# Moving the weight block sums of two seven-product feed-forwards from VectorE to GpSimd

## The reference, cut to what matters

```python
h = rmsnorm(x, norm_ffn[layer])
x = x + (jax.nn.silu(h @ w_gate[layer]) * (h @ w_up[layer])) @ w_down[layer]
```

## Time and profile before

| what | value |
|---|---|
| median of 3 runs | 2076.34 us (2073.32 to 2083.42) |
| the profiled execution: own time | 2077.95 us |
| its span | 2076.2 us |
| mean granted TensorE clock | 0.896 |
| PE busy | 1702.6 us (82%) |
| DVE busy | 706.7 us (34%) |
| ACT busy | 359.4 us (17%) |
| POOL busy | 79.9 us (4%), all before 580 us |
| DMA | 381.57 MB, mean 184 GB/s |

### The profile page before, as it was taken

One profiled execution on the slowest core, in us unless ns is written; L12 is line 12 of the kernel. 1 busy time (PEld: TensorE's weight loads), 2 busy tenths in 40 slices (PEclk: granted clock), 3 DMA queues, 4 the chain that ended last, 5 costly groups with the idle time before them and its releaser, 6 DMA issues.

```text
span 2076.2 us, 31931 instructions
## 1 busy us (share of the span) xinstructions
PE 1702.6 (82%) x14144; PEld 1154.0 (56%) x14144; DVE 706.7 (34%) x1255; ACT 359.4 (17%) x832; POOL 79.9 (4%) x85
## 2 busy tenths in 40 slices
PE   6999889969978585556555688989999889899997
PEld 3665458848962251122111256657994466659963
DVE  2005473362340410000000024464664243546663
ACT  2010213232321220000000022421010124310000
POOL 0000004203300000000000000000000000000000
PEclk7999999978998797788778898989999989899999
DMA  9431120000004959999999961213545522134450
GB/s 375 180 122 41 65 82 3 3 1 3 4 3 182 397 245 427 428 427 428 428 428 428 427 230 47 102 56 116 209 169 197 194 101 82 41 122 168 175 196 21
DMA packets 35164, 381.57 MB, mean 184 GB/s; under 512 B 6674, under 2 KB 10130, under 8 KB 12242
## 3 DMA queue, kind: packets, MB, share of 16 engines
q1 hardware_dynamic: 35028, 379.53, 45.7%
HBM read 378.46 MB, written 1.05 MB: 183 GB/s over the span
## 4 chain that ended last, share of the span: by engine, by line
PE 48%; DMA 11%; DVE 4%; ACT 2%; issue 1%; SPq 0%; DVEq 0%; ACTq 0%
PE psum L2619 14%; PE psum L1764 7%; PE psum L2690 7%; DMA arena<-in_w_moe 6%; PE psum L2055 5%; DMA weight_ring<-in_w_moe 5%; PE psum L2058 3%; PE psum L2210 3%; PE psum L1726 3%; PE psum L2186 1%; PE psum L2165 1%; PE psum L1706 1%; PE psum L2074 0%; ACT arena L2262 0%; PE psum L2151 0%
## 5 line engine op out<-in xcount | busy, mean ns | idle before, releaser
L1764 PE MATMUL psum<-weight_ring,arena 128*32 128x512 f32 x640 | 142.6, 716 | 126.5 <-DMA arena<-in_w_moe 92.2
L1188 PE MATMUL psum<-arena 64*64 64x64 f32 x4608 | 151.4, 223 | 20.3 <-PEq L945 8.2
L2619 PE MATMUL psum<-arena 128*128 128x128 f32 x1408 | 165.2, 275 | 1.7 <-DVE arena L2822 1.7
L2619 PEld LDWEIGHTS psum<-arena 128*128 128x128 f32 x1408 | 161.1, 192 | 2.0 <-issue 2.0
L1188 PEld LDWEIGHTS psum<-arena 64*64 64x64 f32 x4608 | 143.7, 138 | 28.2 <-issue 24.2
L1764 PEld LDWEIGHTS psum<-weight_ring,arena 128*32 128x32 f32 x640 | 35.9, 129 | 204.9 <-issue 204.9
L1899 DVE COPY arena<-psum 128x512 f32<-128x512 f32 x16 | 11.1, 692 | 370.3 <-PE psum L1764 370.3
L2619 PE MATMUL psum<-arena,weight_ring 128*128 128x128 f32 x1056 | 131.9, 283 | 4.7 <-ACT arena L2736 2.6
L1764 PE MATMUL psum<-arena 128*32 128x512 f32 x384 | 107.4, 726 | 34.3 <-DMA weight_ring<-in_w_moe 33.9
L2619 PEld LDWEIGHTS psum<-arena,weight_ring 128*128 128x128 f32 x1056 | 127.3, 199 | 5.9 <-DVE arena L2867 3.1
L2055 PE MATMUL psum<-arena,weight_ring 128*128 128x256 f32 x512 | 123.8, 401 | 0.0
(11 more groups left out here) (491 smaller groups left out, 2250.1 us busy)
## 6 DMA issues: line engine op xcount, KB each, us to landing
weight_ring<-in_w_moe SPq DMA_DIRECT2D x60, 2048.0 KB, 20.2
arena<-in_w_moe SPq DMA_DIRECT2D x36, 2048.0 KB, 20.2
weight_ring<-in_w_in SPq DMA_DIRECT2D x23, 2048.0 KB, 8.4
weight_ring<-in_w_mod SPq DMA_DIRECT2D x12, 2048.0 KB, 8.7
weight_ring<-in_w_gate SPq DMA_DIRECT2D x12, 2048.0 KB, 8.0
weight_ring<-in_w_up SPq DMA_DIRECT2D x12, 2048.0 KB, 7.6
weight_ring<-in_w_down SPq DMA_DIRECT2D x12, 2048.0 KB, 7.6
weight_ring<-in_w_out SPq DMA_DIRECT2D x6, 2048.0 KB, 8.0
```

The lines of the kernel that those rows point to most:

```text
L1188: last = nc.tensor.matmul(K.ps[half[d], bank, column + HD * n:column + HD * n + HD], lhs(d, h), rhs(d, h), start=True, stop=True, skip_gro ...
L1764: last = nc.tensor.matmul(K.ps[strip(j), 4, :], xsT[:, k, CAP * e:CAP * e + CAP], ws[j][:, k, :], start=(k == 0), stop=(k == KT - 1), skip ...
L2619: last = nc.tensor.matmul(K.ps[:, bank, P * n:P * n + P], lhs, rhs, start=(n == 0 and k == 0 and name in ("m1", "m5", "m6")), stop=(k == 3 ...
```

## The change

The sums are issued by GpSimd from a program of its own in this block, slot after slot, all 18 of a layer, from the point at which the mixer's output is ready. DVE's queue loses them: the two early slots at the end of the mixer, the four between the evictions of a unit, and the rest behind the last unit. The formulas and the widths are the same. The wait on the buffer is now on product m3 of slot v - 2; the wait on the landed weights moves with the sums.

```diff
-    def block_sum(dve, v, n):
-        if v >= UNITS + FCH:
-            return
+    def block_sum(pool, v, n):
         slot = START + v
         to = block_sums[:, v % 2]
         if n == 0:
-            W.await_landed(dve, slot)
+            W.await_landed(pool, slot)
             if v >= 2:
-                dve.wait_ge(made, 7 * (v - 1) if v <= UNITS + 1 else 7 * UNITS + v - UNITS - 1)
+                pool.wait_ge(made, step["m3", v - 2] if v <= UNITS + 1 else 7 * UNITS + v - UNITS - 1)
...
         if n in (1, 3):
-            dve.wait_ge(sums_ready, 4 * v + (1 if n == 1 else 2))
+            pool.wait_ge(sums_ready, 4 * v + (1 if n == 1 else 2))
         out, x, y, op = ops[n]
-        nc.vector.tensor_tensor(out, x, y, op).then_inc(sums_ready, 1)
-
-    def early_sums(dve):
-        for v in range(2):
+        nc.gpsimd.tensor_tensor(out, x, y, op).then_inc(sums_ready, 1)
+
+    def gpsimd(pool):
+        pool.wait_ge(K.shared("o_ready"), layer + 1)
+        for v in range(UNITS + FCH):
             for n in range(4):
-                block_sum(dve, v, n)
+                block_sum(pool, v, n)
...
-            if u:
-                block_sum(dve, u + 1, 0)
...
-        for v in range(UNITS + 1, UNITS + FCH):
-            for n in range(4):
-                block_sum(dve, v, n)
-
...
             @block.gpsimd
             def _(pool):
-                pass
+                feed_0[4](pool)
+                feed_1[4](pool)
```

More of the change, by code:

```diff
@@ L2325, in scalar, with vector @@
             item(name)
-    def vector(dve, meanwhile):
+    def vector(dve):
         link = chain(dve, dve_step)
@@ L2543, in vector @@
         ins.then_inc(o_ready, 1)
-        meanwhile(dve)
         for t in range(TT):
@@ L2828, in unit @@
             nc.vector.tensor_tensor(to[2], bank(2), u3[:, par, 0:n], ALU.add).then_inc(took, 1)
-            if u:
-                block_sum(dve, u + 1, 1)
             if par:
@@ L2835, in unit @@
                 nc.vector.tensor_tensor(opened, bank(0), gate[:, c % 2, 0, 0:n], ALU.mult).then_inc(hid_opened, 1)
-            if u:
-                block_sum(dve, u + 1, 2)
             dve.wait_ge(made, step["m4", u])
             nc.vector.tensor_tensor(to[1], bank(1), first[:, par, 0:n], ALU.add).then_inc(took, 1)
-            if u:
-                block_sum(dve, u + 1, 3)
             dve.wait_ge(made, step["m3", u])
@@ L2921, in feed_forward @@
     A.high = top
-    return sync, tensor, scalar, vector, early_sums
+    return sync, tensor, scalar, vector, gpsimd
 def experts_and_layers(nc, K):
@@ L2954, in _ @@
             def _(dve):
[L2955 to L2959, removed]
+                for part in parts:
+                    part[3](dve)
 def first_and_second_block(nc, dram, out):
```

## The result

The changed kernel takes 2164.55 us in the median of 4 runs (2161.51 to 2173.31), the kernel before 2079.88 (2073.32 to 2089.35, 4 runs): a ratio of 1.041, 95% interval 1.0357 to 1.0464. It is slower, at 2165 where 2169 was forecast. The profiled execution took 2164.4 us with a span of 2162.6, which is 86.4 us more than before. The two feed-forwards account for more than that.

The account below looks back on a forecast made before the run. TensorE runs nearly without a break; 5.7 us per layer could be blamed on DVE. Meeting 30.2, clock 13 and pace 3.3 make 46.5 us per layer, 93 for both: 2171 profiled, 2169 us median, range 2082 to 2190.

Parts of the forecast that it names:

- The meeting of the two engines: At odd units' ends GpSimd's sums start while DVE closes the chunk, delaying TensorE's eviction: 30.2 us per layer.
- the upper bound: Each of DVE's five chunk-closing instructions waits for the sum in progress: TensorE loses 6.6 us, 3.8 at unit 10.
- one path for both operands of GpSimd: GpSimd's 2.13 ns per element against DVE's 1.2, read as fetching two operands one after the other.
- The clock: TensorE's granted clock falls behind each of five gaps per layer: 2.6 us per gap, 13 us per layer.
- the tail: Last two down slots: 0.5 us more clock loss per layer behind a longer gap.
- GpSimd's pace: Slower sums delay the first down slot by 0.7 to 1 us and the last two by 1.8.
- What was free was free: Early slots' sums finish before TensorE wants them; four sums, 8.7 us, fit a 12.5 us unit: no cost.
- No contention: Rival: at chunk ends the engines do not delay each other; 3.3 us per layer, 2083 us, chance 0.18.
- blocked once: Rival: at chunk ends DVE waits for the first sum, then runs its five through; 2085 us, chance 0.10.
- half blocked: Rival: at chunk ends DVE gets its turn after two sums, not four; 2118 us, chance 0.13.
- The other side: Rival: GpSimd's 1024-wide sum takes 1.22 us and nothing contends; first down-slot gap goes; 2072.6 us, chance 0.04.

Follow-up runs that it names:

- e5: Changed kernel with one operand of each of VectorE's five chunk-closing instructions taken from an idle PSUM bank: 2087.95 us, ratio 1.0041 to the kernel before.
- e1: Changed kernel with GpSimd waiting before the sums of an odd slot until VectorE has closed the chunk before it: 2093.52 us, ratio 1.0082 to the kernel before.

## Why the prediction was right

**The meeting of the two engines.** The step that I chose without a row for it, the upper bound, was the right one: all four sums run ahead of L2820. The reason that I took from the rows, that 2.13 ns per element point to one path for both operands of GpSimd, is still only a reading: the experiments show which accesses meet, not how GpSimd fetches them. Its size: 4 x 6.2 us and 3.6 more at unit 10 (4.45 against 0.83), 28.5 us per layer for the 30.2 forecast. Two errors went against each other. A 1024-wide sum takes 2.35 us, not 2.18. But a short VectorE instruction between two sums adds less than its own length: with one between them the sums start 2.49 us apart (1451.77 to 1454.26) against 2.31 without (e5: 1446.94 to 1449.26), so 0.18 us for one of 0.42.

**The clock.** Forecast 13.0 us per layer behind the five gaps and 0.5 more in the tail; the lengths leave 12.3 and 1.3. One full gap seen by itself cost 2.5 us, for the 2.6 I took.

**GpSimd's pace.** Forecast 0.7 to 1 us at the first down slot and 1.8 at the last two; measured 1.8 and 2.4. The mis-sized term is the sum's length: 2.35 us wide and 1.26 narrow, where I doubled the 1.09 of the scan. At the first place L2838 and L2843 of unit 11 took turns with the last sums as well.

**What was free was free.** The early slots' sums started at 1388.2 us, and TensorE waited for none of them; throughput holds at 9.4 us of sums for a 12.5 us unit, as e1 shows.

**The rivals.** No contention would have meant about e5's 2088 us for the changed kernel, and not the 2083 of the prediction, which had GpSimd's pace too short and no clock behind it; blocked once and half blocked have fallen by the four stretched instructions. The other side, a wide sum of 1.22 us, fell with 2.35.

The steps add up to 28.5 + 13.6 + 1.8 + 2.4 = 46.3 us per layer, the mean of the two layers, for 46.5 forecast. So near a hit is partly luck: the meeting was 1.7 us too dear, the two places of the pace 1.4 us too cheap (4.2 us where 2.8 were forecast at most). That the time came out 4 us under the forecast is no term of the sum. The two profiled executions differ outside the feed-forwards as well, most of all at the start of the mixer, where TensorE stood nearly idle for 4.5 us in both (0.7 us of matmuls). Windows behind that pause, before and after (columns as in the earlier trace rows):

```profile
1638.40:1646.00 7.60, 7.59 (x17) 3.70 (x18) 1.49 (x4) 1.14 (x3) 0.00 (x0) 0.60 0.97 411
```

```profile
1683.80:1691.00 7.20, 7.16 (x23) 3.79 (x24) 1.77 (x4) 2.32 (x7) 0.00 (x0) 1.00 0.99 422
```

Why the granted clock fell in one and not in the other stays open.

## What to carry to other kernels

Before work goes to GpSimd, list what VectorE runs at that moment by its operands: an instruction with two SBUF inputs, or a fast one with one, takes turns with each GpSimd instruction that reads SBUF. Here that cost up to 6.2 us of gap a chunk, and the 81 us a layer taken off VectorE gave nothing back, since they lay beside the matmuls. If the work must go there, start it at an event at which VectorE only evicts from PSUM, or put it in shorter pieces. And ask first whether the waits blamed on the busy engine can be met by awaiting later: moving three waits in TensorE's queue brought 0.75%, the moved load nothing.

## What the runs showed of the hardware

- Turns are one instruction each, also where the next one of GpSimd waits for nothing. The waiting shows as length, on GpSimd too (2.94 and 2.52 us for 2.35).
- A 512-wide sum on GpSimd took 1.26 us in the feed-forward and 1.09 in the scan, whole and undisturbed in both. The operands differ in layout and source; why it is so stays open.
- TensorE's granted clock behind a gap: full after 3.7 us ahead of the first down slot, 0.57 over 4 us after 4.6 us there (e1), 0.54 over 3.5 us after 3.0 us ahead of the last two. At the start of the mixer it was 0.60 or 1.00 behind the same pause of 4.5 us. The length of the gap alone does not decide.
